# A two-block layer in fp32: more seven-product steps in the q, gate and last output groups, and the last column block in halves

## The reference

```python
x = x + rmsnorm(fox_attention(rmsnorm(x, g0)), g1)
x = x + rmsnorm(square(relu(rmsnorm(x, g2) @ w1)) @ w2, g3)        # w1: 2048x8192, w2: 8192x2048
```

```python
h = rms_norm(x, norm_g); proj = h @ w_in
y_a = (moba_attention(norm(q), norm(k), v) * silu(z_a)) @ w_proj_a
y_b = (spatial_gating(gelu(u_b), gelu(v_b)) * silu(z_b)) @ w_proj_b
out = x + (sigmoid(g_a) * y_a + sigmoid(g_b) * y_b) @ w_out
```

## Time and profile before

| | us |
|---|---|
| median of 3 runs (1764.12 to 1764.59) | 1764.49 |
| the profiled execution's own time | 1763.71 |
| its span, first to last instruction | 1762.0 |
| PE busy (100%) | 1753.5 |
| DVE busy (77%) | 1363.8 |
| ACT busy (53%) | 933.8 |
| POOL busy (13%) | 226.2 |

### The profile page before, as it was taken

The page is one execution under the profiler, slowest core; times in us unless marked ns, Lnnn a source line. Parts: engine busy times, 40 slices in busy tenths (PEclk is TensorE's granted clock), DMA queues, the critical chain, the costliest instruction groups (busy, mean ns, idle before and its releaser), DMA issues.

```text
span 1762.0 us, 24213 instructions
## 1 busy us (share of the span) xinstructions
PE 1753.5 (100%) x8731; PEld 1487.1 (84%) x8731; DVE 1363.8 (77%) x1786; ACT 933.8 (53%) x1283; POOL 226.2 (13%) x294
## 2 busy tenths in 40 slices
PE   9999999999999999999999999999999999999999
PEld 8888888888888888888888887788888888888887
DVE  6567777556799779878987887899888656885797
ACT  7434444446556446545654555767654455654453
POOL 1024434111000200110011000020003011000000
PEclk9999999999999999999999999999999999999999
DMA  9787777886867976787688676566655645565566
GB/s 330 249 274 216 233 224 228 265 263 193 242 207 232 263 235 218 228 273 226 217 235 278 202 225 220 178 213 195 203 187 180 200 159 166 191 201 193 179 198 185
DMA packets 108505, 387.81 MB, mean 220 GB/s; under 512 B 13136, under 2 KB 13536, under 8 KB 107232
## 3 DMA queue, kind: packets, MB, share of 16 engines
q1 hardware_dynamic: 93392, 333.23, 56.7%
q0 software_dynamic: 14160, 52.98, 12.9%
q10 hardware_dynamic: 864, 0.44, 0.1%
HBM read 376.10 MB, written 41.44 MB: 237 GB/s over the span
## 4 chain that ended last, share of the span: by engine, by line
PE 95%; DVE 3%; ACT 1%; issue 0%; POOL 0%; ACTq 0%; DVEq 0%; POOLq 0%
PE bank L508 23%; PE bank L529 22%; PE bank L513 12%; PE bank L823 11%; PE bank L825 11%; PE bank L824 11%; PE bank L579 1%; PE bank L545 1%; DVE w_lo L1721 1%; PE bank L658 1%; PE bank L701 1%; PE bank L716 1%; ACT w_hi L1140 1%; PE bank L707 0%; PE bank L700 0%
## 5 line engine op out<-in xcount | busy, mean ns | idle before, releaser
L1721 DVE TENSOR_TENSOR w_lo<-raw,w_hi 128x1024 fp32r<-128x1024 f32 x620 | 752.6, 1227 | 267.1 <-ACT w_hi L1140 263.1
L1140 ACT ACTIVATE w_hi<-raw 128x1024 fp32r<-128x1024 f32 x620 | 649.9, 1055 | 480.9 <-PE bank L529 183.3
L508 PE MATMUL bank<-h_both,w_hi 128*128 128x512 f32 x1792 | 432.6, 394 | 0.0
L508 PEld LDWEIGHTS bank<-h_both,w_hi 128*128 128x128 f32 x1792 | 330.7, 188 | 65.1
L513 PEld LDWEIGHTS bank<-h_both,w_lo 128*128 128x128 f32 x1792 | 229.8, 191 | 8.7
L513 PE MATMUL bank<-h_both,w_lo 128*128 128x256 f32 x1792 | 232.5, 283 | 0.0
L529 PE MATMUL bank<-w_hi,h_both 128*128 128x512 f32 x648 | 204.0, 396 | 0.0
L529 PE MATMUL bank<-w_hi,a_both 128*128 128x512 f32 x576 | 178.4, 391 | 0.0
L529 PEld LDWEIGHTS bank<-w_hi,h_both 128*128 128x128 f32 x648 | 119.8, 188 | 23.7
L529 PE MATMUL bank<-w_lo,h_both 128*128 128x512 f32 x324 | 126.8, 391 | 0.0
L529 PEld LDWEIGHTS bank<-w_hi,a_both 128*128 128x128 f32 x576 | 107.7, 188 | 22.0
(11 more groups left out here) (300 smaller groups left out, 2266.5 us busy)
## 6 DMA issues: line engine op xcount, KB each, us to landing
raw<-in_stream SPq DMA_DIRECT2D x572, 512.0 KB, 4.3
summed<-in_stream POOLq DMA_DIRECT2D x50, 512.0 KB, 7.6
raw<-summed SPq DMA_DIRECT2D x50, 512.0 KB, 4.3
summed<-in_stream POOLq DMA_DIRECT2D x50, 256.0 KB, 6.9
wide<-scaled POOLq DMA_DIRECT2D x21, 256.0 KB, 4.9
res<-in_x SPq DMA_DIRECT2D x4, 512.0 KB, 7.4
rowg<-in_norm_rows POOLq DMA_DIRECT2D x2, 1024.0 KB, 9.0
gate<-cum_rows POOLq DMA_DIRECT2D x1, 2048.0 KB, 9.3
```

The lines of the kernel that those rows point to most:

```text
L508: pe.matmul(tile_sum[b][:, :], w_hi[:, slot + half, k * P:(k + 1) * P], h_both[:, 8 * half + k, :], start=half == 0 and k == 0, stop=False)
L1140: nc.scalar.activation(w_hi[:, slot, :], raw[:, slot, :], ACT.Copy).then_inc(hi_ready, 1)
L1721: nc.vector.tensor_tensor(w_lo[:, slot, :], raw[:, slot, :], w_hi[:, slot, :].bitcast(F32), ALU.subtract).then_inc(lo_ready, 1)
```

## The change

The layouts get names. q and both gate groups go from three steps to four, the last output group from two to three, with its own order of pairs. `SUMMED` grows from 50 to 54 chunks. `rstd_sq` moves behind the second step of MLP group 0. One `h_forms` moves ahead into the norm's boundary, the others and their `hi`/`lo` are spread. The gates get a fourth input form. In the last output group block 3 is closed early (its bank is added at once), the last four chunks go into two half banks of 256 columns, and the last block is added and stored in two pieces.

```diff
-PAIR_ORDERS = {2: (0, 1, 4, 2, 5, 3, 6, 7), 3: (0, 1, 4, 2, 5, 3, 6, 7), 4: (0, 1, 4, 5, 2, 6, 7, 3)}
-STEPS_AT = {2: (4, 8), 3: (4, 8, 12), 4: (4, 6, 10, 12)}
-FORMS_LATE = (6, 12)
+Layout = collections.namedtuple("Layout", "at late order")
+THREE = Layout((4, 8, 12), (), (0, 1, 4, 2, 5, 3, 6, 7))
+FOUR = Layout((4, 6, 10, 12), (6, 12), (0, 1, 4, 5, 2, 6, 7, 3))
+LAST = Layout((4, 6, 10), (6,), (0, 1, 4, 5, 2, 6, 3, 7))
...
-GROUP_STEPS = [STEPS] * WIDE_GROUPS + [3, 4, 4] + [3, 3] + [3, 2]
+LAYOUTS = [FOUR] * WIDE_GROUPS + [FOUR] * QKV_WIDE + [FOUR, FOUR] + [THREE, LAST]
+GROUP_STEPS = [len(layout.at) for layout in LAYOUTS]
...
-X_STEPS = (STEPS, 3, 3)
+X_STEPS = (STEPS, STEPS, 3)
+LAST_PIECES = ((0, 0, 512), (1, 0, 512), (2, 0, 512), (3, 0, 256), (3, 256, 256))
...
+BLOCK_CLOSED = N_CHUNKS - RING - 3
# PE, last_chunks
-                for j in ring:
-                    block_product(j, 3).then_inc(chunk_done, 1)
+                pe.wait_ge(join_step, 8 * (OUT_FIRST + 1) + 4)
+                for half in range(2):
+                    for j in ring:
...
+                        mm = product(half_bank[half][:, 0:TOK], x_block, w_half, j == ring[0], j == ring[-1])
+                        if half:
+                            mm.then_inc(chunk_done, 1)
+                    if half == 0:
+                        mm.then_inc(third_done, 1)
# ACT
+                    if w == 1 and j == 0:
+                        act.wait_ge(rstd_sq_ready, 1)
...
-                if g == 0:
-                    act.wait_ge(rstd_sq_ready, 1)
...
-                if m >= 2:
-                    h_forms_hi(0, m - 2)
-            h_forms_hi(0, 2)
-            h_forms_hi(0, 3)
+                if m in (0, 2):
+                    h_forms_hi(0, m // 2)
...
             vb_squares(0)
+            h_forms_hi(0, 2)
             vb_split(0, 2)
             vb_split(0, 3)
+            h_forms_hi(0, 3)
             vb_in(1)
# DVE, MLP group 0
+                    if w == 0 and q == 1:
+                        dve.wait_ge(rstd_ready, 2)
+                        nc.vector.tensor_tensor(rstd_sq[:, :], rstd[:, :], rstd[:, :],
+                                                ALU.mult).then_inc(rstd_sq_ready, 1)
...
                     scale_of_rows(1)
-                    dve.wait_ge(rstd_ready, 2)
-                    nc.vector.tensor_tensor(rstd_sq[:, :], rstd[:, :], rstd[:, :],
-                                            ALU.mult).then_inc(rstd_sq_ready, 1)
-                    dve.wait_ge(rstd_sq_ready, 1)
# DVE, boundary and start of qkv
                     next_rest(e + 12 + m)
+                    if norm == 2 and m == 2:
+                        h_forms(0, 0)
...
             scale_of_rows(2)
-            h_forms(0, 0)
+            h_forms(0, 1)
             next_rest(c + 9)
-            h_forms(0, 1)
+            h_forms_lo(0, 0)
+            h_forms(0, 2)
             next_rest(c + 10)
             diagonal(3)
-            h_forms(0, 2)
+            h_forms_lo(0, 1)
             next_rest(c + 11)
-            h_forms_lo(0, 0)
-            h_forms(0, 3)
-            for q in range(1, STEPS):
-                h_forms_lo(0, q)
...
             vb_totals(0)
+            h_forms_lo(0, 2)
             next_rest(c + 14)
+            h_forms(0, 3)
             next_rest(c + 15)
+            h_forms_lo(0, 3)
...
             vb_cubes(1, 1)
-            next_rest(c + 18)
-            vb_gelus(1)
-            next_rest(c + 19)
+            wide_step(WIDE_GROUPS, 1, qkv_forms, between=lambda: vb_gelus(1))
...
-                    if i == 0 and q == 1:
+                    if i == 0 and q == 2:
                         vb_totals(1)
# DVE, gates
-            next_rest(c + 2)
             h_forms_lo(1, 1)
-            moba_gated(MOBA_LAST)
-            next_rest(c + 3)
+            wide_step(GATES_FIRST, 1, gate_forms[0], between=lambda: moba_gated(MOBA_LAST))
             h_forms_lo(1, 2)
             moba_att_lo(MOBA_LAST)
+            h_forms(1, 3)
             for i in range(GATE_WIDE):
...
+                    if i == 0 and q == 2:
+                        h_forms_lo(1, 3)
# DVE, last output group
-            rests(c + WIDE_CHUNKS + 8, range(2))
             join_seven(w + 1, o_seven[1], h_part)
             for t in range(NT):
                 rest(c + WIDE_CHUNKS + 10 + t, 2 + t)
...
+            dve.wait_ge(chunk_done, BLOCK_CLOSED + 1)
+            nc.vector.tensor_tensor(h_part[3], h_part[3], o_bank[1][3][:, :], ALU.add).then_inc(res_joined, 1)
# POOL
-            sum_chunks(28, FIRST["mlp"], range(14, 26, 3))
+            sum_chunks(28, FIRST["mlp"], range(14, 29, 3))
...
-                    sum_chunks(29 + 3 * w - 3, WIDE_FIRST[w] - 32, range(2, 26, 4))
+                    sum_chunks(33 + 7 * (w // 2 - 1), WIDE_FIRST[w] - 32, range(2, 30, 4))
```

More of the change, by code:

```diff
@@ L75 @@
     WIDE_FIRST += [FIRST[_name] + _at + WIDE_CHUNKS * i for i in range(_n)]
-SUMMED = [first + at for first, n in zip(WIDE_FIRST, GROUP_STEPS) for at in STEPS_AT[n][:n]]
+SUMMED = [first + at for first, layout in zip(WIDE_FIRST, LAYOUTS) for at in layout.at]
 HEAD_CHUNKS = 16
@@ L158, in build @@
         probT = sb("probT", [P, 384])
+        q_head_base = nc.sbuf_base
         q_head = sb("q_head", [P, TOK])
@@ L218, in build, with by_step @@
         x_form_raw = spare[:, 1536:2048].rearrange("p (f t) -> p f t", f=4)
-        mlp_forms = Forms(form_raw, form_hi, form_lo, x_form_raw, x_form_hi, x_form_lo, addend)
+        def by_step(parts):
+            return [parts[:, q, :, :] for q in range(parts.shape[1])]
+        mlp_forms = Forms(form_raw, form_hi, form_lo, x_form_raw, by_step(x_form_hi), by_step(x_form_lo), addend)
         def in_a(name, at, shape, dt=F32R):
@@ L225, in build @@
         h_part = [gate_flat[:, 2048 + n * 512:2560 + n * 512] for n in range(4)]
-        h_raw = [h_part[q % 3 + 1].rearrange("p (f t) -> p f t", f=4) for q in range(STEPS)]
+        h_raw = [part.rearrange("p (f t) -> p f t", f=4) for part in (*h_part[1:4], h_part[1])]
         h_sum = [gate_flat[:, 2048 + b * 256:2304 + b * 256] for b in range(2)]
@@ L838, in wide_chunk @@
                         x_block = [part[:, kt, t * P:(t + 1) * P] for part in x]
-                        mm = product(plain[2 * t + n], x_block, w_block(j % RING, n), first, last)
+                        closed = last or c + j == BLOCK_CLOSED and t == 1 and n == 1
+                        mm = product(plain[2 * t + n], x_block, w_block(j % RING, n), first, closed)
                     if last and t == 0:
@@ L855, in x_form @@
                 def x_form(f):
-                    return [part[:, q, f, :] for part in (forms.x_hi, forms.x_lo)]
+                    return [part[q][:, f, :] for part in (forms.x_hi, forms.x_lo)]
                 pe.wait_ge(lo_ready, c + j + 1)
@@ L894, in wide_pairs @@
                         seven_blocks(c, j, steps[j], w, plain, seven, x, forms, x_formed)
-                        if GROUP_STEPS[w] == STEPS and j in FORMS_LATE:
+                        if j in LAYOUTS[w].late:
                             held.append(steps[j])
@@ L1018, in last_chunks @@
                 mm.then_inc(third_done, 1)
-                for j in ring:
-                    block_product(j, 3).then_inc(chunk_done, 1)
+                pe.wait_ge(join_step, 8 * (OUT_FIRST + 1) + 4)
+                for half in range(2):
+                    for j in ring:
+                        kt = 2 * pair_at(OUT_FIRST + 1, j) + j % 2
+                        x_block = [part[:, kt, P:2 * P] for part in (h_hi, h_lo)]
+                        at = GROUP_COLS + half * TOK
+                        w_half = [part[:, j % RING, at:at + TOK] for part in (w_hi, w_lo)]
+                        mm = product(half_bank[half][:, 0:TOK], x_block, w_half, j == ring[0], j == ring[-1])
[3 more added lines that the diff above has]
+                        mm.then_inc(third_done, 1)
             first_groups(FIRST["mlp"], 4, 1)
@@ L1397, in wide_split @@
             def wide_split(w, j, forms, seven):
-                late = FORMS_LATE if GROUP_STEPS[w] == STEPS else ()
+                late = LAYOUTS[w].late
                 next_split(WIDE_FIRST[w] + j)
@@ L1481, in h_forms_hi @@
                 forms = x_forms_at[stage]
-                nc.scalar.activation(forms.x_hi[:, q, :, :], forms.x_raw[q], ACT.Copy).then_inc(x_form_hi_ready, 1)
+                nc.scalar.activation(forms.x_hi[q], forms.x_raw[q], ACT.Copy).then_inc(x_form_hi_ready, 1)
             for m in range(4):
@@ L2140, in wide_step @@
                 c, at = WIDE_FIRST[w], steps[q][1]
-                early = 3 if GROUP_STEPS[w] == STEPS and at in FORMS_LATE else 2
+                early = 3 if at in LAYOUTS[w].late else 2
                 upto = steps[q + 1][1] if q + 1 < len(steps) else at + RING
```

122 lines of the change are left out of this document (65 added, 57 removed).

## The result

The kernel after takes **1766.91 us** in the median of 20 runs (1766.02 to 1769.64), the kernel before 1764.20 (1763.79 to 1765.55, 20 runs beside them): a ratio of **1.0017, 95% interval 1.0011 to 1.0024**, 2.7 us longer, within 0.2% as forecast. The profiled execution took 1766.02 and spans 1764.3 us, where the one before spans 1762.0.

A forecast was written before the change was run, and what follows sets the result against it. PE, busy all the time, was taken to bound the kernel. MLP group 0 -0.93, q +0.7, gates +0.4, last output group +2.6 and end -0.3 made +2.5 us on a median of 1764.5: 1767.0, range 1760.0 to 1769.2.

The forecast's parts named there:

- The likeliest case: The main forecast: +2.5 us, 1767.0, within 0.2%; its own range 1765.3 to 1768.6, chance 0.56.
- rstd_sq, -0.93: MLP group 0: with DVE's wait for POOL's power one step later, chunk 6's residual is in time, saving 0.93 us.
- q's old waits, -1.73: Start of q: moved input forms remove PE's losses of 1.20 for chunk 16's residual and 0.53 for the scale rows' copy.
- products, -2.73: q, gates and last output group: four products fewer on PE, 0.68 us each, saving 2.73 if nothing waits.
- q, 3.1 of waits: PE waits for residuals, split and forms in q: chunk 22 1.0, chunk 23 0.97, chunk 24 0.4 and 0.55, last step 0.2.
- The collision: In q one DVE input-form sum takes 1.06 instead of 0.29 beside POOL's select; this 0.77 was expected to stay.
- Gates, 1.8: First gate group: PE waits 0.2 us at chunk 10 and 1.6 at chunk 12; second group 0.
- Last output group, 3.3: PE waits 2.25 us before chunk 14 and 1.03 before chunk 15, whose residuals stand behind the join and additions of res.
- End, -0.3: Last block in halves: matmuls +0.14 us, last sum -0.24, smaller store -0.2.
- A: Rival: DVE gets ahead enough everywhere and all is covered; -5.7 us, 1758.8, faster; chance 0.12.
- B: Rival: only the last output group's wait of 3.3 us comes; -2.4, 1762.1, same; chance 0.17.
- C: Rival: late loads bind in q and the gates from about 5 us; 1769 at 6 us, over 0.2% slower; chance 0.15.

The follow-up runs named there:

- experiment 4: The kernel after without its four new steps, each group in its old order; rstd_sq's move, q's moved input forms and the halved end kept: 1760.75 us, 0.9981.
- moves_and_end: The kernel of experiment 4: the kernel after without its four new steps, keeping the moves and the halved end; 1760.75 us, 0.9981.
- stores_held: two_new with the four stores of the last output group's first output columns held until the last chunk's split: 1759.77 us, 0.9974.
- experiment 2: The kernel after with three steps in q again and v_b's gelus where they were before; moved input forms kept: 1764.51 us, 1.0003.
- q_three: The kernel of experiment 2: the kernel after with three steps in q and v_b's gelus back in their old place; 1764.51 us, 1.0003.
- Experiment 6: The kernel of experiment 1 with v_b's second-half gelus behind the form residual of q's second step, ACT's squares two splits later: 1763.26 us, 0.9996.
- q_relieved: The kernel of experiment 1 with v_b's cubes, gelus and reductions on DVE later, ACT's tanhs and squares later, POOL's select behind q: 1764.44 us, 1.0002.
- experiment 1: The kernel after with the residuals of chunks 14 and 15 of the last output group ahead of the join: 1763.59 us, 0.9997.
- late_join: two_new with the residuals of chunks 14 and 15 of the last output group behind the join again, as in the kernel after: 1764.20 us, 1.0001.
- two_new: The kernel of experiment 1 with q and the first gate group at three steps again, each in its order of before: 1760.27 us, 0.9978.
- experiment 5: The kernel of experiment 1 with the last block whole again, one 512-column sum and one 256 KB store: 1764.07 us, 0.9999.
- gelus_later: The kernel of Experiment 6: that of experiment 1 with v_b's gelus behind the form residual of q's second step; 1763.26 us, 0.9996.
- one_late: two_new with only chunk 15's residual behind the last output group's join: 1761.22 us, 0.9984.

## Why the prediction was right, and where its steps were not

The likeliest case came, with nearly its sum (+2.5 forecast; +2.3 on the spans, +2.7 on the medians). That it came so close is in part luck: q's waits were put 0.3 too low, the clock was left out, and against that the end was put 0.4 and the last group's waits 0.2 too high. Each gap stood at a place named beforehand; those with a releaser are ended by `w_lo` or, in one case, by the form residual.

- *rstd_sq, -0.93; q's old waits, -1.73; products, -2.73:* right. The first two are in the rows after and in experiment 4 (3.4 with the end's 0.5 to 0.7); for a product, the profiles of moves_and_end and stores_held differ by 1.4 for two.
- *q, 3.1 of waits:* the trace has 2.93, and 0.5 for slow first matmuls, which the sum left out. Taking the step away gained 2.4 (experiment 2), which is 3.1 of waits for a product of 0.68 (in the traces the stretch up to the attention is 2.9 shorter, and q_three's clock fell in more of its runs). The amount was right, **the reason half**: that chunk 23's 0.97 "depends only on the order" is wrong. Experiment 6 removed just that order, the gap went and came back at chunk 28. DVE is busy from 1117 to 1179 but for 1.3 us in three short waits, and a step adds 1.86 of sums and 1.68 of residual = 3.5 to it; PE waits 3.4 for it, for a product of 0.68 saved.
- *The collision:* I left the 0.77 in; the sum took 1.06 again. In q_relieved, with POOL's select elsewhere, the same sum took 0.29, and two residuals (1184.52), one beside the select and one beside the POOL sum behind it, took 3.20 instead of 2.35. The Trainium skill, "SBUF — State Buffer", Who interferes with whom, says that a VectorE instruction with two SBUF inputs and a GpSimd one that reads SBUF lock each other out for a whole instruction; these rows agree.
- *Gates, 1.8:* 1.62, and 1.84 with the slow first matmuls. That the second group costs nothing was right too: no gap there.
- *Last output group, 3.3:* 2.92, or 3.1. The order was the cause (experiment 1), as said; but "nothing hides these" was only true of the order as written, since DVE had been idle for 3.04 before the join. And the median pays more than the profile: late_join against two_new costs 3.9. The sum left out the clock, and that the last load lands late in some executions.
- *End, -0.3:* 0.7 by the two traces, 0.5 by experiment 5. The term of the store was mis-sized: 0.45 to 0.54 in the profiles instead of 0.2.
- *Rivals:* A and B needed cover for the steps, which DVE didn't have in q and the gates. Of C, loads that come late as the steps crowd, nothing showed in q or the gates.

What stays open: where two_new's two gaps in the MLP come from, why the last load lands late in some executions, and what decides in which runs the clock falls after PE's stop.

## What to carry to other kernels

Before moving matmul work into a helper engine's sums, add up that engine's work over the whole stretch up to the next place where it has idle time: where it has next to none, nearly all that is added comes back as waits of PE (here 3.5 added, 3.4 waited), and reordering moved the loss more than it shrank it (0.3 less in one order, 0.85 more in another). Where it does have idle time, look for what stands behind a waiting instruction though its inputs are ready; two residuals moved ahead of one join were worth 3.3 us here. And make the parts of a combined change separately: six microseconds of loss hid a gain of three.

## What the runs showed that I had not expected

- A stop of PE of 2.1 us or more was followed, in 7 of 20 to 9 of 11 runs of the kernels that had one in the last output group, by a mean clock under 1.000; in the profiles that caught it by 3 us at 0.50, where each matmul of 512 columns cost 0.2 more. The six new kernels with gaps of at most 1.5 us showed it in 1 run of 63, the kernel before in 2 of 105. In between lie gelus_later with a gap of 1.9 in q (1 of 11) and one_late (2.19 in its profile, 3 of 11).
- The last load of 512 KB landed 4.7 to 6.7 us after its issue in the twelve profiles whose last output group has the layout of the kernel after. A load 1.2 us later than usual made PE's gap 3.0 instead of 2.1 (late_join). Whether the four stores right behind it on the same queue cause that is open.
- In the wide groups, the first matmul after a loss of 0.2 us or more at full clock takes 0.08 to 0.12 longer to be followed by the next.
- POOL's work moved elsewhere met other instructions of DVE there: 1.05 us in k (q_relieved) for 0.77 won at the start of the phase.
